# GpSimd does the post work of the gate/up products, packed gate/up loads, another order of TensorE's rows

## What is computed

```
D_MODEL, SEQ, D_FF = 2048, 512, 5632
x = x + einsum('bse,ed->bsd', mix, w_out)          # mix: both attention groups, normed
h = rmsnorm(x, ffn_norm)
gate = einsum('bsd,df->bsf', h, w_gate)
up = einsum('bsd,df->bsf', h, w_up)
x = x + einsum('bsf,fd->bsd', silu(gate) * up, w_down)
return rmsnorm(x, final_norm)
```

## Time and profile before

| what | us |
|---|---|
| median of 3 runs (2033.5 to 2035.97) | 2033.67 |
| the profiled execution | 2032.2 |
| its span | 2030.4 |
| TensorE busy | 2013.3 (99%) |
| VectorE busy | 1528.3 (75%) |
| ScalarE busy | 1005.3 (50%) |
| GpSimd busy | 142.7 (7%) |
| DMA queue q1 (SyncE), share of 16 engines | 36.8% |

### The profile page before, as it was taken

One profiled execution on the slowest core, in us unless ns is written; L12 is line 12 of the kernel. 1 busy time (PEld: TensorE's weight loads), 2 busy tenths in 40 slices (PEclk: granted clock), 3 DMA queues, 4 the chain that ended last, 5 costly groups with the idle time before them and its releaser, 6 DMA issues.

```text
span 2030.4 us, 30889 instructions
## 1 busy us (share of the span) xinstructions
PE 2013.3 (99%) x10492; PEld 1720.2 (85%) x10492; DVE 1528.3 (75%) x2250; ACT 1005.3 (50%) x1874; POOL 142.7 (7%) x235
## 2 busy tenths in 40 slices
PE   9999999999999999999999999999999999999998
PEld 7888888887888988888888888888888888888886
DVE  5666666666766999898999999999998546546446
ACT  6455555554436654555555455554555323333333
POOL 0122222221100000000000000000000000000000
PEclk9999999999999999999999999999999999999999
DMA  8222222224234344444444444444447653544433
GB/s 295 83 75 72 77 72 73 73 72 153 76 99 155 116 139 131 132 138 125 139 137 132 138 137 136 127 141 133 131 138 243 241 179 99 177 154 120 140 96 133
DMA packets 263774, 265.32 MB, mean 131 GB/s; under 512 B 14080, under 2 KB 194560, under 8 KB 262656
## 3 DMA queue, kind: packets, MB, share of 16 engines
q1 hardware_dynamic: 249136, 224.97, 36.8%
q0 software_dynamic: 6336, 23.07, 2.9%
q10 hardware_dynamic: 8208, 15.98, 2.2%
HBM read 232.51 MB, written 31.46 MB: 130 GB/s over the span
## 4 chain that ended last, share of the span: by engine, by line
PE 75%; DVE 10%; issue 7%; ACT 4%; DMA 3%; SPq 1%; ACTq 0%; DVEq 0%; POOLq 0%; POOL 0%
PE bank L556 20%; PE bank L560 10%; PE bank L489 10%; PE bank L490 10%; PE bank L491 10%; PE bank L445 4%; PE bank L447 4%; PE bank L446 4%; DVE t_lo L1533 3%; DMA t_raw<-in_w_up 2%; ACT probs L848 1%; ACT w_hi L805 1%; PE bank L608 1%; DVE part L1542 1%; DVE w_lo L1250 1%
## 5 line engine op out<-in xcount | busy, mean ns | idle before, releaser
L556 PE MATMUL bank<-s_two,t_hi 128*128 128x512 f32 x2352 | 609.9, 392 | 2.7 <-ACT part L1070 1.3
L1250 DVE TENSOR_TENSOR w_lo<-raw,w_hi 128x512 fp32r<-128x512 f32 x364 | 253.2, 697 | 382.0 <-ACT w_hi L805 379.9
L1030 ACT ACTIVATE t_hi<-t_raw 128x1792 fp32r<-128x1792 f32 x176 | 303.3, 1724 | 378.4 <-DVE t_raw L1527 233.2
L556 PEld LDWEIGHTS bank<-s_two,t_hi 128*128 128x128 f32 x2352 | 413.0, 188 | 67.2 <-issue 1.5
L805 ACT ACTIVATE w_hi<-raw 128x512 fp32r<-128x512 f32 x364 | 229.0, 631 | 481.0 <-PE bank L491 354.4
L560 PEld LDWEIGHTS bank<-s_two,t_lo 128*128 128x128 f32 x2352 | 338.2, 190 | 35.4
L1533 DVE TENSOR_TENSOR t_lo<-t_raw,t_hi 128x1792 fp32r<-128x1792 f32 x176 | 355.2, 2018 | 8.4 <-ACT t_hi L1030 8.1
L560 PE MATMUL bank<-s_two,t_lo 128*128 128x256 f32 x2352 | 347.6, 281 | 0.0
L489 PE MATMUL bank<-w_hi,down_hi 128*128 128x512 f32 x640 | 249.1, 389 | 0.4 <-DVE down_lo L1259 0.4
L490 PE MATMUL bank<-w_lo,down_hi 128*128 128x512 f32 x640 | 249.0, 389 | 0.0
L491 PE MATMUL bank<-w_hi,down_lo 128*128 128x512 f32 x640 | 249.0, 389 | 0.0
(11 more groups left out here) (170 smaller groups left out, 2504.4 us busy)
## 6 DMA issues: line engine op xcount, KB each, us to landing
raw<-in_w_down SPq DMA_DIRECT2D x176, 256.0 KB, 3.2
t_raw<-in_w_gate SPq DMA_DIRECT2D x174, 256.0 KB, 3.1
t_raw<-in_w_up SPq DMA_DIRECT2D x174, 256.0 KB, 3.4
raw<-in_w_in SPq DMA_DIRECT2D x136, 256.0 KB, 2.6
gu_s<-gu_mid SPq DMA_DIRECT2D x44, 512.0 KB, 5.3
gu_mid<-part POOLq DMA_DIRECT2D x43, 512.0 KB, 2.9
raw<-in_w_out SPq DMA_DIRECT2D x64, 256.0 KB, 3.2
x_row<-in_x ACTq DMA_DIRECT2D x4, 1024.0 KB, 12.0
```

Source lines behind the costliest of these rows:

```text
L556: nc.tensor.matmul(bank[SEVEN_BANK[i]][:, :], t_hi[r][:, SEVEN[i][0], q, :], both, start=d == 0 and q == 0, stop=False, skip_group_check=True)
L1030: nc.scalar.activation(t_hi[r][:, :, :, :].rearrange("p a q c -> p (a q c)"), t_raw[r][:, 1:8, :, :].rearrange("p a q c -> p (a q c)"), AC ...
L1250: nc.vector.tensor_tensor(w_lo[:, s, :], raw[:, s, :], w_hi[:, s, :].bitcast(F32), ALU.subtract).then_inc(w_lo_done, 1)
```

## The change

- `post` leaves VectorE and stands on GpSimd, just ahead of the store of the same group. Its instructions and sizes are the same.
- w_gate and w_up come from one DRAM tensor w_gu, laid out by the host so that each load of 128 partitions reads 2048 bytes in a row for each (before: four pieces of 512 bytes). The number of loads, their bytes and their waits stay.
- In `double_wide` the order of the matmuls follows WIDE_ORDER. Before, the first and last double of a group went by pairs of products (the 512-column matmuls of two products, then their 256-column ones) and the middle ones by all seven. Now a double runs all its 512-column and all its 256-column matmuls in one piece each (in the last, the 256-column ones of products 0 to 3 come first and those of 4 to 6 last), and where doubles meet, rows of one kind stand next to each other. In the last double, products 0 to 3 are complete after their 512-column matmuls, 4 to 6 after their 256-column ones.

```diff
+WIDE_ORDER = ((("both", 0, QUAD), ("low", 0, QUAD)), (("low", 0, QUAD), ("both", 0, QUAD)),
+              (("both", 0, QUAD), ("low", 0, QUAD)), (("low", 0, 4), ("both", 0, QUAD), ("low", 4, QUAD)))
...
-        for dst, w in ((t_raw[r][:, 0:2, :, :], w_gate2), (t_raw[r][:, 7:9, :, :], w_up2)):
-            yield (dst.rearrange("p j q c -> p (j q) c"),
-                   w[512 * d:512 * (d + 1), bass.ds(g * P, P)].rearrange("(k p) c -> p k c", p=P))
+        four = t_raw[r][:, :, :, :].rearrange("p a q c -> p (a q c)")
+        for i, at in ((0, 0), (1, 7 * HALF)):
+            yield (four[:, at:at + SEQ], w_gu[bass.ds(g, 1), d, i, :, :].rearrange("o p c -> (o p) c"))
...
-            step = QUAD if 0 < d < DOUBLES - 1 else 2
-            for i0 in range(0, QUAD, step):
-                some = range(i0, min(i0 + step, QUAD))
-                for i in some:
...
+            for kind, i0, i1 in WIDE_ORDER[d]:
+                for i in range(i0, i1):
...
+                    if d == DOUBLES - 1 and i < QUAD - 1 and (kind == "both") == (i < 4):
                         mm.then_inc(prod_ready, 1)
...
-                if j % 4 == 3:
-                    post(i, j // 4 - 1)
...
+        def post(g):
+
+            z = part_low if g == 1 else part
+            pool.wait_ge(bank_taken, taken_by(0, g))
+            if g > 1:
+                nc.gpsimd.tensor_tensor(part[:, :, :], part[:, :, :], part_low[:, :, :], ALU.add).then_inc(folded, 1)
+                pool.wait_ge(folded, g - 1)
+            nc.gpsimd.tensor_tensor(z[:, 1, :], z[:, 1, :], z[:, 5, :], ALU.add).then_inc(post_done, 1)
+            nc.gpsimd.tensor_tensor(z[:, 2, :], z[:, 2, :], z[:, 4, :], ALU.add).then_inc(post_done, 1)
+            pool.wait_ge(post_done, POSTS * g + 2)
+            nc.gpsimd.tensor_tensor(z[:, 1:3, :], z[:, 1:3, :], z[:, 0:4:3, :], ALU.add).then_inc(post_done, 1)
+            pool.wait_ge(post_done, POSTS * g + 3)
+            nc.gpsimd.tensor_tensor(z[:, 1:3, :], z[:, 1:3, :], z[:, 6:7, :].broadcast_to([P, 2, HALF]), ALU.add).then_inc(post_done, 1)
+            nc.gpsimd.tensor_tensor(z[:, 0:4:3, :], z[:, 0:4:3, :], z[:, 4:6, :], ALU.subtract).then_inc(post_done, 1)
...
         for g in range(TILES):
+            post(g)
             store_gu(g)
```

More of the change, by code:

```diff
@@ L97, with build @@
 HEAD = [("A", 0, 0), ("A", 1, 3), ("B", 0, 6), ("B", 1, 8)]
-def build(nc, x, x_turned, gain_cols, w_in, sinks, w_out, w_gate, w_up, w_down, final_norm, c_dist, c_lnm, c_band, c_slope, c_ident, x_mid, gu_mid, out):
+def build(nc, x, x_turned, gain_cols, w_in, sinks, w_out, w_gu, w_down, final_norm, c_dist, c_lnm, c_band, c_slope, c_ident, x_mid, gu_mid, out):
     spot = [(nc.sbuf_base + 63) // 64 * 64]
@@ L264, in build @@
     w_out2 = w_out[0]
-    w_gate2, w_up2, w_down2 = w_gate[0], w_up[0], w_down[0]
+    w_down2 = w_down[0]
     x2, out2 = x[0], out[0]
@@ L545, in double_wide @@
             pe.wait_ge(t_lo_done, j + 1)
-            step = QUAD if 0 < d < DOUBLES - 1 else 2
-            for i0 in range(0, QUAD, step):
-                some = range(i0, min(i0 + step, QUAD))
-                for i in some:
-                    if d == 0 and g == 2:
+            for kind, i0, i1 in WIDE_ORDER[d]:
+                for i in range(i0, i1):
+                    ti, si, _ = SEVEN[i]
+                    b = bank[SEVEN_BANK[i]]
+                    if d == 0 and kind == "both" and g == 2:
                         pe.wait_ge(bank_taken, 4 if i < 4 else i + 1)
-                    elif d == 0:
+                    elif d == 0 and kind == "both":
                         pe.wait_ge(bank_taken, taken_by(0, g - 2) + 2 * (i + 1))
                     for q in range(2):
[L555 to L563, removed]
+                        both = s_two[2 * d + q][:, si, :, :].rearrange("p a c -> p (a c)")
+                        if kind == "both":
+                            mm = nc.tensor.matmul(b[:, :], t_hi[r][:, ti, q, :], both, start=d == 0 and q == 0,
+                                                  stop=d == DOUBLES - 1 and q == 1 and i < 4, skip_group_check=True)
+                        else:
+                            mm = nc.tensor.matmul(b[:, 0:HALF], t_lo[r][:, ti, q, :], both[:, 0:HALF], start=False,
+                                                  stop=d == DOUBLES - 1 and q == 1 and i >= 4, skip_group_check=True)
+                    if d == DOUBLES - 1 and i < QUAD - 1 and (kind == "both") == (i < 4):
                         mm.then_inc(prod_ready, 1)
@@ L1631, in six_groups @@
                 first = isinstance(i, int) and i == 0
-                if first and j == 9:
-                    post(0, 0)
-                if j % 4 == 3:
-                    post(i, j // 4 - 1)
                 if first and j == 14:
@@ L1688, in down @@
                     down_low(0, s + 2)
-                if first and s == 6:
-                    post(7, 1)
                 if s % 8 < 2:
@@ L1856, in laid_out @@
     w_in = w_in[0].reshape(4, 4, P, IN_COLS // P, P).transpose(3, 0, 2, 1, 4).reshape(IN_COLS // P, 4, P, 4 * P)
-    return {"x_turned": np.ascontiguousarray(x[0].T), "gain_cols": np.ascontiguousarray(np.concatenate(cols, axis=1)),
+    w_gu = np.stack([np.asarray(inputs[name])[0].reshape(DOUBLES, 4, P, TILES, P) for name in ("w_gate", "w_up")])
+    w_gu = w_gu.transpose(4, 1, 0, 3, 2, 5).reshape(TILES, DOUBLES, 2, P, 4 * P)
+    return {"w_gu": np.ascontiguousarray(w_gu), "x_turned": np.ascontiguousarray(x[0].T), "gain_cols": np.ascontiguousarray(np.concatenate(cols, axis=1)),
             "w_in": np.ascontiguousarray(w_in)}
```

18 lines of the change are left out of this document (2 added, 16 removed).

## The result

The changed kernel takes 2149.12 us (median of 5 runs, 2147.02 to 2150.15) against 2033.67: 1.0564 times as long (95% interval 1.0552 to 1.0576), or 115.5 us more. The forecast was 2371 us. It was slower, as forecast, and inside the range, but by a third of the 338 us that were expected; it came out where rival 1 stood, at 2140.

What follows compares the result with a forecast made beforehand. TensorE was taken to bound the kernel at 19.54 us a group; with post on GpSimd a group would take 28.0, so 8.46 us more in about 40 groups, 338 us, giving 2371 us against the median (range 2110 to 2450).

Steps and rivals of the forecast that it cites:

- rival 1: Wide doubles: GpSimd gets in after every VectorE instruction, 22.2 us a group, 2140 us in all; chance 0.19.
- What bounds the kernel: Gate and up doubles: TensorE sets the time at 19.54 us a group, VectorE close behind at 18.4.
- TensorE's order: Wide doubles: 10 pairs of 512/256-column runs a group fall to 3, at 13 ns a pair, 3.9 us gained.
- Packed loads: Gate and up weight loads: 0 gained, bounds 0 to 1.5 us, since loads hardly held TensorE.
- the ring of three slots: Gate and up weight loads: the buffering said to cover their landing time, 3.4 us after issue.
- GpSimd's own times: Post work on GpSimd: six additions at 2.25 ns an element, 8.6 us, or 9.5 us a group with dispatch.
- The exclusion: Wide doubles: VectorE instructions with two SBUF inputs and GpSimd instructions reading SBUF do not run together.
- VectorE keeps the shared read path through a run of ready instructions: Wide doubles: GpSimd enters only where VectorE truly waits, so nearly all work lines up, 28.0 us a group.
- The chain of 28.7 us: One group, last take to last take: fold, VectorE runs, additions, store and takes one after the other; 28.0 taken.
- TensorE at 70% with long waits on ScalarE's takes: Expected sign in the doubles: TensorE's share about 70%, waiting for takes held by GpSimd's last addition and the store.
- Rivals 2 and 3: Wide doubles: additions beside VectorE cost little, 2027 us, chance 0.09; additions fit but bank waits eat the gain, 2030-2037, 0.03.
- Rival 4: Wide doubles: slower fold and store, TensorE below full clock for longer, 29.5 to 31 us a group, 2430-2490 us; chance 0.05.

## Why the prediction was right or wrong

**What bounds the kernel** (right). TensorE bound it with VectorE 1.1 us a group behind, and as soon as VectorE's work and waiting passed TensorE's 19.5 us, it showed in the time.

**TensorE's order** (right in kind, high in size). 13 ns a pair were taken from averages of 4.905 and 4.865 us; it is 10 ns. 3.9 us were forecast and 2.7 came in the doubles, none of it in the time, since waits for banks and loads took it back. In the change it was worth nothing, as forecast. A slip on the way: by its own terms ScalarE's last take ends at 4.9 + 3 x 0.54 = 6.5 us, not 6.2, which is still ahead of the 7.6 us at which the bank is wanted.

**Packed loads** (right for the kernel before, missed for the change). 0 to 1.5 us were forecast, and alone they gave 2. In the changed kernel they give 24.4 us. The cover that I named, the ring of three slots, was the wrong one: the 1.1 us a group by which VectorE was ahead of TensorE covered its waits for loads, and the other part of the change took that away.

**GpSimd's own times** (right). 8.6 us of holding for the six additions were forecast from 2.25 ns an element; VectorE lost 8.20, 3.87 for the 1792 elements, 0.54 for 256, 1.09 for 512, which is 2.1 to 2.2 ns an element. No row shows the 0.15 us of dispatch that made it 9.5: in the trace after, an addition starts at most 0.08 us after the one ahead has ended (1237.32 to 1237.40).

**The exclusion** (right). It reaches these tiles and these additions, in both directions.

**"VectorE keeps the shared read path through a run of ready instructions"** (wrong as the rule, and the step that failed). VectorE's instructions in the doubles stood ready back to back in the trace after, and GpSimd came in after one of them in 242 of 252 additions. Once, in the fold at 764.28, it was as the step has it, for a reason that stays open; the forecast took that for every group. The step rested on two rows. One was an instruction of a form that waits twice, which no addition does, and for the other I set the wrong end against the lone duration. Two instructions that VectorE ran undelayed looked like a run it had kept; they were two turns. I had a row against the step, L1267's 1.73 us, and explained it away by its 64 partitions.

**The chain of 28.7 us** (wrong by that step). Its terms of 5.35 and 6.8 us, where four and six VectorE instructions pass one addition, are not in the median group: the post takes 15.3 us, not some 23. So the store and the takes are hidden, and what is left is the sum of what the two engines hold. The sum stood in the text as rival 1, 22.2 us a group and 2140 us; it was 22.09. The chances were the fault, not the arithmetic: 0.64 to 0.19 on two rows of another form of instruction.

**TensorE at 70% with long waits on ScalarE's takes** (wrong). 93%, its waits are nearly all for t_lo (61.4 of 68.8 us), none is over 1.6 us in the doubles, and the clock of the stretch is 1.00.

**Rivals 2 and 3** (did not come). The exclusion reaches these additions, and nothing fits beside VectorE for nothing. **Rival 4** (did not come up). The store did not come onto the path in the change.

**What no step had.** The last post beside the first down unit: 2.55 us x 42 groups = 107 us explain the 106 of the doubles, and the other 10 lie here, of which the last post explains 8.3: a wait of 6.55 us and 6.7 us at a clock of 0.60. "Each group costs so much, times 40" left out the group whose neighbour is another stage.

## What to carry to other kernels

Before moving work from VectorE to GpSimd, add up per period what VectorE will still do and what GpSimd will read, at GpSimd's price (2.1 to 2.2 ns an element here, against 1.1 on VectorE): if the VectorE work has two SBUF inputs, as all of it has here, the sum must stay below the bound, and GpSimd's idle share says nothing. Here 13.6 + 8.2 replaced 18.4 under a bound of 19.5. Take the witness rows for a contention from the same form of instruction as the one that is moved, and look again at what each hidden wait costs once the engine that hid it is no longer the bound.

## What was unexpected of the hardware

- With both engines queued for the read path they took turns: one VectorE instruction ended during 242 of 252 GpSimd additions, and VectorE waited for one of GpSimd's at a time (4.29 us for 0.42 behind the fold). One fold in each such kernel waited for four, until VectorE had a gap (8.04 us for 3.9), and in the kernel with the fold on VectorE an addition of 0.6 us waited for six (7.26 us).
- GpSimd's scaling of 128x384 took, on average, 3.26 us with its factor in SBUF and 1.33 with constants, among the same VectorE work.
- Alternating 512- and 256-column matmuls costs TensorE 10 ns for each pair of runs (19.540 against 19.473 us a group, seven pairs fewer).
- After a wait of 6.55 us the granted clock was 0.60 over 6.7 us, and after one of 5.53 us it was 0.50 over 5 us; over the doubles of the change, with waits of up to 1.6 us, it was 1.00.
